# Prompt attention tiles of each head group in the order of widths 3, 1, 4, 2 in place of 1, 2, 3, 4

## What is computed

```python
_, idx = lax.top_k(score, min(SLC_TOP_N, nb))        # all 8 blocks
s_s = jnp.einsum('bqgrd,bqgnkd->bqgrnk', qg, ks.astype(f32))
m_s = (pos <= tq[None, :, None, None, None]).reshape(B, Q, G, 1, -1)
p_s = masked_softmax(s_s.reshape(B, Q, G, R, -1), m_s).reshape(s_s.shape)
o_s = jnp.einsum('bqgrnk,bqgnkd->bqgrd', p_s, vs.astype(f32))
...
o = g[..., 0:1] * o_c + g[..., 1:2] * o_s + g[..., 2:3] * o_w
```

## Time and profile before

| | us |
|---|---|
| median of 3 runs | 1359.13 (1359.06 to 1361.33) |
| the profiled execution | 1358.04 |
| its span, first to last instruction | 1356.3 |
| PE, DVE, ACT, POOL busy in the span | 1268.5, 681.8, 433.7, 89.3 |
| mean granted clock of PE | 0.948 |

### The profile page before, as it was taken

One profiled execution on the slowest core, in us unless ns is written; L12 is line 12 of the kernel. 1 busy time (PEld: TensorE's weight loads), 2 busy tenths in 40 slices (PEclk: granted clock), 3 DMA queues, 4 the chain that ended last, 5 costly groups with the idle time before them and its releaser, 6 DMA issues.

```text
span 1356.3 us, 21135 instructions
## 1 busy us (share of the span) xinstructions
PE 1268.5 (94%) x7779; PEld 997.5 (74%) x7779; DVE 681.8 (50%) x1673; ACT 433.7 (32%) x1039; POOL 89.3 (7%) x162
## 2 busy tenths in 40 slices
PE   7999999787998999999999999599999999999995
PEld 4677776673676787778777878378888888788883
DVE  4733423857775656665666552745545545110013
ACT  4000005124666656755675530411111111000003
POOL 4200000011442000000000000100000000000000
PEclk9899997676998999999999999899999999999997
DMA  9534321413003553465343512411222221112201
GB/s 356 212 126 180 130 99 48 162 31 124 2 1 153 236 216 127 186 263 214 127 186 139 206 70 83 156 58 66 94 77 78 93 68 68 64 65 67 82 21 66
DMA packets 21268, 162.63 MB, mean 120 GB/s; under 512 B 2728, under 2 KB 6920, under 8 KB 11032
## 3 DMA queue, kind: packets, MB, share of 16 engines
q1 hardware_dynamic: 18328, 92.42, 18.8%
q0 software_dynamic: 2736, 69.36, 12.3%
q10 hardware_dynamic: 144, 0.04, 0.0%
HBM read 156.73 MB, written 9.24 MB: 122 GB/s over the span
## 4 chain that ended last, share of the span: by engine, by line
PE 86%; DVE 6%; ACT 4%; issue 3%; DMA 0%; POOL 0%; ACTq 0%; DVEq 0%; POOLq 0%
PE PS L313 79%; PE PS L900 4%; PE PS L1074 3%; ACT sreg L1232 1%; DVE ringreg L1788 1%; PE PS L994 1%; ACT zreg L1385 1%; DVE zreg L1898 0%; PE PS L743 0%; DVE creg L1730 0%; ACT zreg L1375 0%; DVE mixreg L1527 0%; ACT trunk L1237 0%; ACT ringreg L1354 0%; DVE zreg L1926 0%
## 5 line engine op out<-in xcount | busy, mean ns | idle before, releaser
L313 PE MATMUL PS<-zreg,ringreg 128*128 128x272 f32 (+1 forms) x736 | 170.4, 394 | 1.9 <-DVE zreg L2086 1.9
L313 PEld LDWEIGHTS PS<-zreg,ringreg 128*128 128x128 f32 x736 | 141.7, 198 | 30.6 <-issue 2.3
L313 PE MATMUL PS<-creg,ringreg 128*128 128x272 f32 (+2 forms) x576 | 149.6, 414 | 12.1 <-issue 8.8
L313 PE MATMUL PS<-zreg,w 128*128 128x256 f32 (+2 forms) x544 | 140.9, 390 | 4.8 <-DVE zreg L1926 2.9
L313 PE MATMUL PS<-mixreg,w 128*128 128x272 f32 (+1 forms) x596 | 135.8, 379 | 6.6 <-DVE mixreg L1723 6.6
L313 PEld LDWEIGHTS PS<-creg,ringreg 128*128 128x128 f32 (+2 forms) x576 | 106.1, 189 | 43.7 <-issue 18.7
L313 PEld LDWEIGHTS PS<-mixreg,w 128*128 128x128 f32 x596 | 107.8, 190 | 27.7 <-DVE mixreg L1723 7.0
L313 PE MATMUL PS<-mixreg,ringreg 128*128 128x272 f32 x520 | 125.0, 393 | 0.5 <-DVE mixreg L1891 0.5
L313 PEld LDWEIGHTS PS<-mixreg,ringreg 128*128 128x128 f32 x520 | 98.6, 190 | 20.8 <-DVE mixreg L1891 0.6
L313 PE MATMUL PS<-zreg 128*128 128x256 f32 (+4 forms) x320 | 105.2, 411 | 5.0 <-DVE ringreg L1800 1.8
L313 PEld LDWEIGHTS PS<-zreg,w 128*128 128x128 f32 (+1 forms) x544 | 90.9, 189 | 22.3 <-issue 5.2
(11 more groups left out here) (340 smaller groups left out, 1759.1 us busy)
## 6 DMA issues: line engine op xcount, KB each, us to landing
ringreg<-in_w_ada_dram SPq DMA_DIRECT2D x24, 1024.0 KB, 6.4
ringreg<-in_w_f_dram SPq DMA_DIRECT2D x22, 1024.0 KB, 4.8
ringreg<-in_w_in_dram SPq DMA_DIRECT2D x11, 1024.0 KB, 4.9
ringreg<-in_w_f_dram SPq DMA_DIRECT2D x16, 704.0 KB, 4.0
sreg<-in_win_dram SPq DMA_DIRECT2D x8, 512.0 KB
ringreg<-in_w_o_dram SPq DMA_DIRECT2D x4, 1024.0 KB, 7.7
out_dram<-in_win_dram SPq DMA_DIRECT2D x1, 4064.0 KB
trunk<-in_x_t_dram SPq DMA_DIRECT2D x4, 544.0 KB, 5.5
```

Of the source, the lines that this page charges most:

```text
L313: return nc.tensor.matmul(o, lhsT, rhs, start=start, stop=stop, **kw)
```

## The change

A tuple gives the order of the query blocks in each group of eight tiles, and each place that worked out j takes it from there. The widths come as 3, 3, 1, 1, 4, 4, 2, 2 in each of the four groups, where they came as 1, 1, 2, 2, 3, 3, 4, 4. The loops, the waits and all instructions stay; where a tile writes its output still goes by its own j.

```diff
         NTL = R * TT * G
+        tile_order = (2, 0, 3, 1)
...
             def scores(t):
-                j, g = t // 2 % TT, t % 2
+                j, g = tile_order[t // 2 % TT], t % 2
...
             def turned(t):
-                j, pb = t // 2 % TT, PB[t % 3]
+                j, pb = tile_order[t // 2 % TT], PB[t % 3]
...
             def values(t):
-                j, g, pt = t // 2 % TT, t % 2, PTB[t % 2]
+                j, g, pt = tile_order[t // 2 % TT], t % 2, PTB[t % 2]
...
             def exponentials(t):
-                j, g = t // 2 % TT, t % 2
+                j, g = tile_order[t // 2 % TT], t % 2
...
-                w = (t // 2 % TT + 1) * P
+                w = (tile_order[t // 2 % TT] + 1) * P
...
             def prepare(t):
...
-                j, g = t // 2 % TT, t % 2
+                j, g = tile_order[t // 2 % TT], t % 2
...
             def finish(t):
...
-                j, g = t // 2 % TT, t % 2
+                j, g = tile_order[t // 2 % TT], t % 2
...
             def output(t):
-                j, g = t // 2 % TT, t % 2
+                j, g = tile_order[t // 2 % TT], t % 2
```

## The result

The first comparison, six runs of each kernel, gave a median of 1365.88 us (1362.5 to 1368.27) against 1359.1 us (1358.7 to 1361.56), a ratio of 1.0042, 95% interval 1.0023 to 1.0061: slower, by 6.8 us where 3.4 were forecast, and outside the stated range. Two later comparisons with more runs gave 1.0015 (0.9999 to 1.0031) and 1.0023 (1.0007 to 1.0039). Over these and a comparison of the kernel before with itself, the kernel before has a median of 1361.5 us (76 runs, 1358.4 to 1368.0) and the changed kernel one of 1364.8 us (30 runs, 1361.5 to 1368.5): 3.3 us, 0.24%. So there are two questions: what the change costs, and where the other 3 us of the first comparison came from.

What follows compares the result with a forecast made beforehand. TensorE, busy in 94% of the span, was taken as the bound, with waits for copies and VectorE's chain in the stage. 3.6 - 0.5 - 0.3 + 0.6 = +3.4 us on 1359.13 gave 1362.5 us, range 1359.7 to 1364.6.

Steps and rivals of the forecast that it cites:

- The mechanism and its place: Step from width 1 to 4: TensorE waits before the first width 4 turned for VectorE's prepares and finish; net +3.6 us.
- The size of the chain: VectorE and GpSimd from scores(20) to turned(20): 6.78 us against 5.57 of TensorE work, 1.21 us waiting in each group.
- The copies: values waiting for ScalarE's second copy, covered only by scores(t+2): waits of 1.53 us after, 2.04 before; net -0.5 us.
- the end: The stage's last three values, with no scores in front, wait 1.83 us after, 2.15 before; net -0.3 us.
- The start: Stage's beginning at the lower clock: first turned 1.9 us later, 1.3 us of scores already done; net +0.6 us.
- Behind the stage: Sample phase after the last output moves along with the stage's delay: counted 0, with 1 us to either side.
- The rivals on the clock: At the stage's start the clock rises earlier, 1360.7 us (chance 0.17), or later, 1364.2 us (0.08).
- The faster side: Step from 1 to 4: queued wide-tile work on TensorE covers the chain; -1.4 us, 1357.7 us; chance 0.06.
- the partly covered chain: Step from 1 to 4: the wait is only about 0.8 us a group; 1360.9 us; chance 0.14.
- The earlier clock: Stage's start: two longer first scores release the full clock near 330 us; 1.8 us back, 1360.7 us; chance 0.17.
- The later clock: Stage's start: pauses keep half speed a third longer, 3.4 us, costing 1.7 us more; 1364.2 us; chance 0.08.

Runs made afterwards that it cites:

- the run with the start undone: Against the changed kernel: widths 1, 2, 3, 4 in the first group, 3, 1, 4, 2 in the other three; single timed run 1367.22 us, stage 102.01 us.
- the shortened maximum: Against the changed kernel: maximum of width 4 tiles taken over their first 128 columns only; median 1361.52 us, groups of 22.69 us.

## Why the prediction was right, and where it was wrong

- **The mechanism and its place were right.** The excess stands where it was put: in front of the first turned of width 4, behind VectorE's two wide prepares (0.84 us there, 0.52 at the narrow turned before; forecast 0.7 and 0.5). The stage ended at 431.55 us where 430.5 was forecast, 0.58 of it from ahead of the stage, and its end and all behind it moved by the same 4.5 us.
- **The size of the chain was a little low.** Forecast: 6.78 us of chain, 1.21 of waiting. Measured: 6.93 and 1.36, the same at all four steps from 1 to 4. The term that was short is finish and output, taken as 0.28 + 0.60 from one row of each; in the profile after they take 1.03 us together (391.09 to 392.12). Over four steps that is the 0.6 us between the forecast +3.4 and the stage's +3.96: 4 x 1.36 - 3 x 0.40 = +4.2 in place of +3.6.
- **The copies and the end were right.** The last three values of after wait 0.75, 0.54 and 0.54 us (weight loads at 425.36, 428.01 and 430.23, behind turned steps that began at 422.62, 426.38 and 428.60).
- **The start was right in its delay, not shown in its cost.** The first turned begins 5.88 us after the first scores in place of 3.98, 1.9 us later as forecast. Its net cost is 0.6 us by the stage's +3.96 less the other terms, and 0.3 by the run with the start undone.
- **Behind the stage: right for this change, not for its 1 us.** Nothing was added there in the three profiles of the changed kernel. But six profiles of edited kernels gained 1.9 to 2.7 us there, more than the 1 us that the prediction allowed for the place of the clock.
- **The failing step is the level from which the sum was counted, and with it the range.** The prediction added +3.4 to the median of three runs, 1359.13 us, and gave the result "its own spread of some 1 us". The runs showed in its place that the kernel before goes from 1358.4 to 1368.0 us with a median of 1361.5, and the changed one from 1361.5 to 1368.5; the execution that was profiled, 1358.04 us, lies below all 76. The spread arises outside the stage: one profile of the same program enters it 4.7 us later than another. The rivals on the clock looked for a difference at the stage's start and missed the larger ones at 20 to 63 us and 245 to 310 us, where the two programs are the same. The range has a slip besides: its lower end takes the 1 us off in full (1360.7 - 1), its upper end adds 0.4 to 1364.2; in full it would be 1365.2, still short of the first 1365.88.
- **Where luck comes in.** On the median of 76 runs the same sum gives 1364.9 us, and 30 runs of the changed kernel gave 1364.8. So close an agreement is luck, since medians of one program lay 2.3 us apart, and the sum itself was 0.6 short of the stage. That the first comparison gave 6.8 us in place of some 3 to 4 is, as far as the runs show, the draw of its twelve executions.
- **The rivals.** The faster side and the partly covered chain fall: each step from 1 to 4 costs its 1.36 us. The earlier clock did not come in three profiles of the changed kernel (10.8, 11.0 and 11.6 us after the first scores, against 10.3 in the profile of before); it came for 3.4 us in one of the same start (below). The later clock came in these three, by 0.5 to 1.3 us in place of 3.4, but an unchanged execution had it too (11.3 us).

## What to carry to other kernels

In a pipeline with fixed orders, sort neighbours by the engine that prepares the next tile, not by the one that is busiest: here a wide tile behind two narrow ones left TensorE without the work that would hide VectorE's long prepare (1.36 us of waiting), while widths that grow by one step left 0.40 us. Count such a wait as chain minus cover, from the row of one step's start to the row of the next; here it came out within 0.15 us. And ahead of a forecast of a quarter of a per cent, look at how far single runs of the unchanged kernel lie apart: three runs that agree within 0.2% don't yet show it.

## What was not expected of the hardware

Executions of one program differ by up to 9.6 us of 1360, mostly with the stretches in which the clock is granted at 0.50. And the clock can rise and fall again within a start: in the profile of the shortened maximum, whose first scores are the changed kernel's and start at 327.56 us, the granted clock was 0.50 until 331.0 us, 1.00 until 334.4, and 0.50 again until 337.8, while the changed kernel itself kept 0.50 throughout such a start in three profiles. The three windows (columns as in the earlier trace rows):

```profile
327.56:331.01 3.45, 2.93 (x8) 1.24 (x8) 1.69 (x4) 0.24 (x2) 0.00 (x0) 0.50 0.74 313
331.01:334.43 3.42, 1.48 (x12) 1.29 (x13) 2.81 (x10) 2.39 (x9) 1.44 (x3) 1.00 1.04 450
334.43:337.84 3.41, 3.41 (x23) 2.63 (x22) 1.34 (x6) 1.67 (x6) 1.04 (x3) 0.50 0.76 327
```

What decides it in one execution and not in another stays open.
